# Where the operands lie in SBUF: weight slots and operand regions moved by a few bytes

## The reference

```python
x = x + 0.5 * ((silu(h @ w_gate) * (h @ w_up)) @ w_down)       # h = rmsnorm(x), hidden width 2816
z = rmsnorm(x) @ w_in                                          # one combined projection
x = x + concat(window_attention(z), gated_linear_scan(z)) @ w_out
x = x + 0.5 * ((silu(h @ w_gate2) * (h @ w_up2)) @ w_down2)
x = rmsnorm(x)
```

## Time and profile before

| | |
|---|---|
| median of 3 runs | 1949.27 us (1944.7 to 1949.57) |
| the profiled execution | 1950.25 us, of which the instructions' span 1948.7 us |
| matmul engine busy | 1927.9 us, 99% |
| weight loads | 1885.3 us, 97% |
| VectorE, ScalarE, GpSimd busy | 66%, 40%, 54% |
| granted TensorE clock, mean | 0.997 of 2.4 GHz |
| chain that ended last | 94% TensorE |

### The profile page before, as it was taken

The page is one execution under the profiler, slowest core; times in us unless marked ns, Lnnn a source line. Parts: engine busy times, 40 slices in busy tenths (PEclk is TensorE's granted clock), DMA queues, the critical chain, the costliest instruction groups (busy, mean ns, idle before and its releaser), DMA issues.

```text
span 1948.7 us, 39225 instructions
## 1 busy us (share of the span) xinstructions
PE 1927.9 (99%) x14627; PEld 1885.3 (97%) x14627; DVE 1279.4 (66%) x1882; ACT 783.2 (40%) x1595; POOL 1051.0 (54%) x958
## 2 busy tenths in 40 slices
PE   8999999999999999999999999999999999999998
PEld 7999999999999999999998999999999999999997
DVE  7766776666466778854445664866767667646674
ACT  6433333333443345733334542443333333344343
POOL 2277776775777641321222442237767776676770
PEclk9999999999999999999999999999999999999999
DMA  8135455344986530333332735214454444498552
GB/s 270 45 114 181 135 168 173 132 133 155 317 309 190 168 100 20 116 113 92 97 103 62 208 98 119 78 56 144 147 181 145 132 154 164 152 355 277 167 156 103
DMA packets 226846, 293.88 MB, mean 151 GB/s; under 512 B 16616, under 2 KB 158472, under 8 KB 226736
## 3 DMA queue, kind: packets, MB, share of 16 engines
q1 hardware_dynamic: 219040, 272.76, 43.8%
q0 software_dynamic: 7696, 19.63, 3.2%
HBM read 198.07 MB, written 94.21 MB: 150 GB/s over the span
## 4 chain that ended last, share of the span: by engine, by line
PE 94%; DMA 2%; DVE 2%; issue 1%; ACT 1%; POOL 1%; SPq 0%; ACTq 0%; POOLq 0%
PE bank L292 29%; PE bank L294 29%; PE bank L293 28%; PE bank L2584 1%; PE bank L2603 1%; PE bank L2594 1%; DMA WRAW<-in_w_down 1%; DMA XIN<-in_x_prompt 1%; DMA ZO<-zm 1%; PE bank L2515 0%; PE bank L1333 0%; PE bank L1335 0%; PE bank L1334 0%; PE bank L1329 0%; PE bank L846 0%
## 5 line engine op out<-in xcount | busy, mean ns | idle before, releaser
L292 PE MATMUL bank<-HA,HW 128*128 128x272 f32 x1120 | 322.4, 288 | 0.6 <-DVE HW L1382 0.6
L294 PE MATMUL bank<-HA,HW 128*128 128x272 f32 x1120 | 322.6, 288 | 0.0
L293 PE MATMUL bank<-HA,HW 128*128 128x272 f32 x1120 | 322.0, 287 | 0.0
L1382 DVE SCALAR_TENSOR_TENSOR HW<-WRAW,HW 128x512 fp32r<-128x512 f32 x140 | 221.2, 1617 | 108.7 <-ACT HW L1377 108.4
L1388 POOL TENSOR_TENSOR HA<-ARAW,HA 128x544 fp32r<-128x544 f32 x140 | 220.7, 1591 | 104.9 <-ACT HA L1376 104.5
L292 PE MATMUL bank<-HH,WGH 128*128 128x362 f32 (+2 forms) x784 | 256.4, 327 | 0.0
L294 PE MATMUL bank<-HH,WGL 128*128 128x362 f32 (+2 forms) x784 | 247.0, 315 | 1.9 <-issue 1.9
L293 PE MATMUL bank<-HL,WGH 128*128 128x362 f32 (+2 forms) x784 | 247.0, 315 | 0.0
L294 PE MATMUL bank<-FC,WR 128*128 128x272 f32 x768 | 222.1, 289 | 0.0
L292 PE MATMUL bank<-FC,WR 128*128 128x272 f32 x768 | 220.9, 288 | 0.6 <-DVE WR L584 0.5
L293 PE MATMUL bank<-FC,WR 128*128 128x272 f32 x768 | 219.8, 286 | 0.0
(11 more groups left out here) (384 smaller groups left out, 5667.6 us busy)
## 6 DMA issues: line engine op xcount, KB each, us to landing
asp<-SA SPq DMA_DIRECT2D x44, 544.0 KB, 3.5
RAWG<-in_w_gate SPq DMA_DIRECT2D x22, 1024.0 KB, 6.5
RAWU<-in_w_up SPq DMA_DIRECT2D x22, 1024.0 KB, 6.4
tsp<-TT SPq DMA_DIRECT2D x40, 544.0 KB, 6.5
ARAW<-tsp SPq DMA_DIRECT2D x80, 272.0 KB, 3.4
WS<-in_w_down SPq DMA_DIRECT2D x20, 1024.0 KB, 8.7
wsp<-WS SPq DMA_DIRECT2D x20, 1024.0 KB, 8.5
WRAW<-wsp SPq DMA_DIRECT2D x80, 256.0 KB, 4.4
```

The source lines that it names most:

```text
L292: nc.tensor.matmul(bank[:, 0:w], w_hi, rhs_hi, start=first, stop=False)
L293: nc.tensor.matmul(bank[:, 0:w], w_hi, rhs_lo, start=False, stop=False)
L294: return nc.tensor.matmul(bank[:, 0:w], w_lo, rhs_hi, start=False, stop=last)
L1382: nc.vector.scalar_tensor_tensor(out=HW[f][h][:, 1], in0=WRAW[r][:, :], scalar=0.5, in1=HW[f][h][:, 0].bitcast(F32), op0=ALU.mult, op1=ALU ...
```

## The change

Only addresses change. The regions stand in another order: `wg` first (at 0, 64 bytes longer), then `raw`, `d`, `t`, the constants, and after pads of 8, 32 and 16 bytes `a`, `hl`, `x` and `hh`. With the sizes in the code `a` and `hl` lie 40 past a multiple of 64, `x` 8 past and `hh` 24 past. (The words that came with the change name 8, 40 and 56 for the operand regions; 24 is what the sizes give for `hh`.) `WR` becomes a list of slots at 4, 12, 20, 28, 36, 44, 52 and 52 past. `WGH` and `WGL` lie 8 past. The pairs of down slots get offsets (`HA`, `HW`) of (8, 0), (8, 32) and (32, 0). Small constants are packed to save room. All uses follow the new names.

```diff
-WEIGHTS = 24
+CONSTANTS = 5408
...
-        rX = region("x", KT * T * 4)
-        rHH = region("hh", KT * T * 4)
-        rHL = region("hl", KT * T * 4)
-        rA = region("a", 4 * T * 4)
-        region("lead", WEIGHTS)
-        rWG = region("wg", 2 * 4 * 4096)
-        region("rest", 32 - WEIGHTS)
+        rWG = region("wg", 2 * 4 * 4096 + 64)
         rRAW = region("raw", 4 * 4096)
         rD = region("d", 3 * 8192)
         rT = region("t", 8 * NW * 4)
-        rC = region("c", 0)
-        assert base + rC < nc.sbuf_usable_end
+        rC = region("c", CONSTANTS)
+        region("before_a", 8)
+        rA = region("a", 4 * T * 4)
+        rHL = region("hl", KT * T * 4)
+        region("before_x", 32)
+        rX = region("x", KT * T * 4)
+        region("before_hh", 16)
+        rHH = region("hh", KT * T * 4)
+        assert base + at["end"] <= nc.sbuf_usable_end
...
-        WGH = place("WGH", [P, 4, KT, P], F32R, rWG)
-        WGL = place("WGL", [P, 4, KT, P], F32R, rWG + 4 * 4096)
+        WGH = place("WGH", [P, 4, KT, P], F32R, rWG + 8)
+        WGL = place("WGL", [P, 4, KT, P], F32R, rWG + 4 * 4096 + 8)
...
-        WR = place("WR", [P, PRODUCTS + 1, 2, 4, P], F32R, rWG)
-        SS = place("SS", [P, 2, 4, P], F32, rWG + PRODUCTS * 4096)
+        WR = [place(f"WR{o}", [P, 2, 4, P], F32R, rWG + 4096 * o + lead) for o, lead in enumerate((4, 12, 20, 28, 36, 44, 52, 52))]
+        SS = place("SS", [P, 2, 4, P], F32, rWG + PRODUCTS * 4096 + 64)
...
-        slot_at = [[rHL, rHL + 8480, rHL + 17408, rHL + 17408 + 8480, o_ + 17408, o_ + 26112] for o_ in (rX, rHH)]
-        HA = [[place(f"HA{f}{h}", [P, 2, 2, HT], F32R, slot_at[f][h]) for h in range(SLOTS)] for f in range(2)]
-        HW = [[place(f"HW{f}{h}", [P, 2, 512], F32R, slot_at[f][h] + 4352 + WEIGHTS) for h in range(SLOTS)] for f in range(2)]
+        slot_at = [[rHL, rHL + 8576, rHL + 17408, rHL + 17408 + 8576, o_ + 17408, o_ + 26112] for o_ in (rX, rHH)]
+        places = ((8, 64), (8, 32), (32, 64))
+        HA = [[place(f"HA{f}{h}", [P, 2, 2, HT], F32R, (slot_at[f][h] + 63) // 64 * 64 + places[h // 2][0]) for h in range(SLOTS)] for f in range(2)]
+        HW = [[place(f"HW{f}{h}", [P, 2, 512], F32R, (slot_at[f][h] + 63) // 64 * 64 + 4352 + places[h // 2][1]) for h in range(SLOTS)] for f in range(2)]
...
-            nc.vector.tensor_tensor(WR[:, o, 1], weight(o, q0, mat), WR[:, o, 0].bitcast(F32), ALU.subtract).then_inc(s_.lo, 1)
+            nc.vector.tensor_tensor(WR[o][:, 1], weight(o, q0, mat), WR[o][:, 0].bitcast(F32), ALU.subtract).then_inc(s_.lo, 1)
...
-                    mm = three_pass(BANK[o], HT, WR[:, o, 0, k], WR[:, o, 1, k], product(o, j, 0, k, f), product(o, j, 1, k, f), k == 0, k == 3)
+                    mm = three_pass(BANK[o], HT, WR[o][:, 0, k], WR[o][:, 1, k], product(o, j, 0, k, f), product(o, j, 1, k, f), k == 0, k == 3)
```

More of the change, by code:

```diff
@@ L209, in build @@
         GC = small("GC", [3, KT])
-        GQ = small("GQ", [2])
-        GO = small("GO", [LH])
+        gains = small("GQOE", [2 + LH + 1])
+        GQ, GO, EPSC = gains[:, 0:2], gains[:, 2:2 + LH], gains[:, 2 + LH:3 + LH]
         SINK = small("SINK", [HEADS])
         NSINK = small("NSINK", [HEADS])
[L214 to L220, removed]
+        gates = small("GATES", [5])
+        GATE, GBF = gates[0:LH, 0:4], gates[0:32 + LH, 4:5]
+        tops = small("TOPS", [8])
+        NMX, SUM = tops[:, 0:4], tops[:, 4:8]
+        sums = small("SUMS", [8])
+        ESK, DEN = sums[:, 0:4], sums[:, 4:8]
         FS = small("FS", [4, 4])
@@ L225, in build @@
         RMB = small("RMB", [NB + 1, LH])
-        assert base + small_at <= nc.sbuf_usable_end
+        assert small_at <= rC + CONSTANTS
         BANK = [ctx.enter_context(nc.psum_tensor(f"bank{i}", [P, 512], F32)) for i in range(8)]
@@ L578, in weight_high @@
                 act.wait_ge(s_.mm, p * 28 + (280 * f - 28 + 14 * mat - 7 + o + 1))
-            nc.scalar.activation(WR[:, o, 0], weight(o, q0, mat), ACT.Copy).then_inc(s_.hi, 1)
+            nc.scalar.activation(WR[o][:, 0], weight(o, q0, mat), ACT.Copy).then_inc(s_.hi, 1)
         def weight_low(dve, f, p, mat, o, first=False):
@@ L961, in start_weight_high @@
                 act.wait_ge(z.mm, C1 + 48 + OUT_STEPS - 4 + i % 4 + 1)
-            nc.scalar.activation(WR[:, i, 0], first_weight(i), ACT.Copy).then_inc(st.whi, 1)
+            nc.scalar.activation(WR[i][:, 0], first_weight(i), ACT.Copy).then_inc(st.whi, 1)
         def start_weight_low(dve, f, i):
             dve.wait_ge(st.whi, 8 * f + i + 1)
-            nc.vector.tensor_tensor(WR[:, i, 1], first_weight(i), WR[:, i, 0].bitcast(F32), ALU.subtract).then_inc(st.wlo, 1)
+            nc.vector.tensor_tensor(WR[i][:, 1], first_weight(i), WR[i][:, 0].bitcast(F32), ALU.subtract).then_inc(st.wlo, 1)
         def start_chain(pe, f, mat, j, i, between=None):
@@ L987, in start_chain @@
                 for k in range(4):
-                    mm = three_pass(BANK[i], HT, WR[:, slot, 0, k], WR[:, slot, 1, k], product(PLACE[e], j, 0, k, f), product(PLACE[e], j, 1, k, f),
+                    mm = three_pass(BANK[i], HT, WR[slot][:, 0, k], WR[slot][:, 1, k], product(PLACE[e], j, 0, k, f), product(PLACE[e], j, 1, k, f),
                                     kh == 0 and k == 0, kh == 1 and k == 3)
```

## The result

The changed kernel takes 1973.03 us (median of four runs, 1972.7 to 1973.68), the kernel before 1948.11 us in the same comparison (four runs, 1944.7 to 1949.57). The ratio is 1.0136, with a 95% interval of 1.0122 to 1.0151: slower by about 25 us. The prediction had 1925 us and an 80% range that ends at 1966, so it was wrong in sign.

What follows compares the result with a forecast made beforehand. TensorE's matmul issue intervals were taken to bound the kernel. Terms -15.0 - 10.4 + 0.8 = -24.6 us; 1950.25 - 24.6 - 1.0 (profiled run over median) = 1924.7, say 1925 us, 80% range 1890 to 1966.

Steps and rivals of the forecast that it cites:

- part (1): Gate/up, 7488 matmuls on WR: new offsets keep the two streams' boundaries apart, 122.5 ns each, -15.0 us.
- Part (2): Down stages, 3360 matmuls on HA/HW: new slot offsets reach 3.1 ns less each, -10.4 us.
- The good level: Best matmul interval seen before the change, excess 9.2 ns over one period per column, so 122.5 ns at 272 columns.
- Part (3): 2400 matmuls on WGH/WGL: HH's first slice meets equal offsets, 166.5 against 165.0 ns, +0.8 us; the others nothing.
- Parts (4) and (5): ScalarE, VectorE and GpSimd writes to moved addresses, and DMAs into moved regions: taken as nothing, DMA bound +2 us.
- A worse level: FFN operands 8 past a multiple of 16 cost in gate/up and down matmuls: 1966 to 1991 us; chance 0.22.
- Offsets don't decide: Matmul interval level hangs on history, not addresses, so the time stays 1949 us within 5; chance 0.12.
- The rule of separate ports: TensorE reads both operands through separate ports, so no offset matters and the time stays; its case had chance 0.12.
- A better level: Odd multiples of 4 avoid every joint step in gate/up and down: 119.4 ns, -59 us, 1890 us; chance 0.22.
- The writers become the bound: VectorE's writes to odd words in gate/up take over twice as long: +27 us per loop at 2.2 times; chance 0.04.

Runs made afterwards that it cites:

- isolated chains: Layer not computed: TensorE alone runs 272-column (once 512-column) matmul chains over pairs of operand and weight offsets; at 272 columns, 122.2 ns for the fastest first-pass pair.
- the kernels 8 bytes apart: Changed kernel with moving operands 4 bytes further, 1943.68 us, and 4 bytes nearer, 1987.93 us; gate/up and projection weights unmoved.
- the first run: 272-column chains alone, operands 0, 8, ... 56 past a multiple of 64 against weights 0, 4, ... 60 past; all pairs have a mean of 126.2 ns.
- the third: The first run's pairs in another order, operands 128 bytes further and weights 256; the median pair moves by 1.1 ns.
- 16/0: Changed kernel with every operand region 16 past a multiple of 64 and all weights at 0: 1940.16 us; the same pair also ran in chains alone.
- four bytes down: Changed kernel with moving operands 4 bytes nearer, all FFN operands 4 past a multiple of 16, gate/up weight slots unmoved: 1987.93 us.
- slots at 12: Changed kernel with moving operands 4 bytes further, all FFN operands 12 past a multiple of 16, gate/up weight slots unmoved: 1943.68 us.

## Why the prediction was wrong

**Right: what bounds the kernel and what could move.** The time is a sum of issue intervals, only addresses changed, and the loss is all in the intervals: with gaps, waits and clock as before, +2.8 and +2.5 ns x 3024 and +1.3 ns x 3360 in the windows alone.

**Wrong, and the step that failed: part (1).** "I take -15.0, since the level of equal offsets is the one that the new pairs avoid." Behind it stood the claim that two read streams lose time when they cross a boundary on the same element, so that weights at odd multiples of 4 and operands at multiples of 8 could only gain. The isolated chains show no such advantage of odd weight offsets (125.62 against 125.05 ns), and no cost of equal ones (125.5 against 126.2 for all pairs). What sorts the means is the moving operand's own start modulo 16, in all weight offsets: 125.3 at 0, 127.1 to 127.5 at 8. WR's operands went from the one to the other. Forecast 122.5 ns and -15.0 us; measured 127.4 ns in the mean, where it was 124.8, and +19.5 us. That the two streams act jointly was no bad guess: their distance moves single pairs by several ns. But it does so around the mean of the operand's class, and the prediction had no term for the class.

**Part (2), HA/HW.** Forecast -10.4 us, measured +4.3. Two thirds of the slots moved to 8 modulo 16 and one third sits at 0: (2 x 127.3 + 125.4) / 3 = 126.7 ns from the classes, measured 126.8. The good level of 122.5 ns came from one stretch of 14 matmuls. The isolated chains hold such pairs (48/32 at 123.2 ns), but moved by 128 bytes the same pair is at 125.0. A level read in a few dozen matmuls was taken for a property of its two offsets.

**Part (3).** The first slice of HH against weights at 8, in the changed kernel, first and last of 22 starts:

```profile
854.04 0.33 PE L295 MATMUL bank<-HH,WGL 128*128 128x364 f32 x1
...
857.56 0.33 PE L295 MATMUL bank<-HH,WGL 128*128 128x364 f32 x1
```

3.52 us / 21 = 167.6 ns, 165.0 before, forecast 166.5. The slice is slower as forecast. That it is for another reason, 8 modulo 16 and not equality, fits the chains of 272 columns; no run isolated this slice. The term was small, and it stayed small: the 544 matmuls of 364 columns with `WGH` and `WGL` took 1.1 us more.

**Parts (4) and (5)** held: no writer is waited for, and the DMAs are all but without effect, as TensorE's gate/up chains that began at 36.9 us begin 0.4 us later, where the bound was +2.

**The rivals.** "A worse level" is what happened: all FFN regions 8 past a multiple of 16, +15 us priced for WR and +2 for HA/HW, measured +19.5 and +4.3; priced 1966 to 1991 us, measured 1973; its deciding point, a mean above 124.5 ns, is passed. It had a chance of 0.22 and deserved the most. Its row was in hand: 24 was the only operand 8 past a multiple of 16 among the six pairs, and it was at the slow end. The argument against it, that 0/32 was as slow, compared single pairs, which differ by up to 7 ns inside a class. "Offsets don't decide" is refuted by the 44 us between the kernels 8 bytes apart. The rule of separate ports, which the prediction took from the Trainium skill, is not touched by those 44 us, since they hang on the moving operand's own start; what speaks against two streams without effect on each other is that the weights' place alone moves the isolated chains with the operand at 32 between 122.2 and 127.2 ns. "A better level" was not seen: no isolated pair is under 122.2 ns, where it had 119.4, and no pair under 124 ns in the first run is so in the third. "The writers become the bound" was not seen: VectorE's busy time in the loop went from 258.4 to 263.9 of 385 us (267.2 with all offsets taken back).

**On the 16-byte line.** The Trainium skill (SBUF — State Buffer, "Door 1: The DMA port swizzle") says that SBUF is read in 16-byte lines and that each crossing costs. The runs agree with a period of 16 bytes in the means and, for class 4, with a cost that grows with the columns. A count of lines touched, 68 for a start at 0 and 69 for any other here, gives another ranking than the one measured: 12 is the cheapest start and 4 the dearest, and one line more can't grow with the columns. Why 12 is cheap and 4 dear stays open. So does why the distance of the two starts moves a pair within its class, and what moves it besides: 48/32 shows two levels at the same offsets, for which neither the history of a chain nor the longer-range place was tried alone.

## What to carry to other kernels

When a kernel is a gapless row of matmuls, the start of the moving operand within 16 bytes is worth 3% of the issue interval (124.5 to 128.3 ns at 272 fp32r columns), so measure each start class over all partners, in isolation and at both 128-byte phases, before laying out memory: here 12 past a multiple of 16 was best, 4 and 8 worst. Don't generalise from one pair of offsets: the pair varies by as much as the class, and the same offsets past 64 bytes can lie at another distance modulo 256 in the next kernel. To carry a measured pair over, keep that distance and the starts within 32 bytes. A mechanism that would explain a few rows is a guess until one is seen that only it explains; count which property all slow rows share first.

## What the runs showed of the hardware that was not expected

- The mean distance between fp32r matmul starts by the moving operand's start modulo 16: 124.5 (12), 125.3 (0), 127.1 to 127.5 (8), 128.3 ns (4) at 272 columns; 230.2, 231.6, 233.5, 237.3 at 512.
- At 12 modulo 16 the weights' offset hardly matters (most pairs within 0.1 ns of 124.4); in the other classes it moves a pair by up to 4 ns either way.
- A shift of 128 bytes changes a pair (16/0: 123.3 and 125.0 ns, in isolation and in the kernel), but not the class.
- Pairs whose starts both lie 32 bytes further agree within 0.3 ns in 112 of 128 cases; with the operand 32 up and the weights 32 down it is 26 of 128.
- In down stages, VectorE is busy 128.1 us and GpSimd 140.8 with the changed slots (128.3 and 136.5 at four bytes down), against 136.6 and 151.2 with slots at 12, and 136.7 and 151.5 in the kernel before, for the same instructions. The offsets of `HW` alone don't do it, as they are the same in the changed kernel and in the one with slots at 12. Nobody waits for them, so it costs and gives nothing; why is open.
